# One core, a hybrid RWKV-7 / MLA / conv-Fourier / GQA network: where the scan's first inverse estimate is made, and where the norm work of the earlier pair stands

## The reference

```python
def step(S, inp):
    r_t, w_t, k_t, v_t, a_t, b_t = inp
    sa = jnp.einsum('bhij,bhj->bhi', S, a_t)
    S = S * w_t[:, :, None, :] + sa[..., None] * b_t[:, :, None, :] + v_t[..., None] * k_t[:, :, None, :]
    return S, jnp.einsum('bhij,bhj->bhi', S, r_t)
...
mean = jnp.mean(y, axis=-1, keepdims=True)
var = jnp.mean(jnp.square(y - mean), axis=-1, keepdims=True)
y = ((y - mean) * lax.rsqrt(var + GN_EPS)).reshape(B, L, D_INNER)
y = y * ln_w.astype(jnp.float32) + ln_b.astype(jnp.float32)
```

## Time and profile before

| | us |
|---|---|
| median of 3 runs | 2484.78 (2483.58 to 2485.72) |
| the profiled execution | 2485.72 |
| its span, first to last instruction | 2482.9 |
| PE busy in the span | 2190.2 (88%) |
| DVE, ACT, POOL busy | 1329.2, 838.6, 1201.1 |

### The profile page before, as it was taken

One profiled execution on the slowest core, in us unless ns is written; L12 is line 12 of the kernel. 1 busy time (PEld: TensorE's weight loads), 2 busy tenths in 40 slices (PEclk: granted clock), 3 DMA queues, 4 the chain that ended last, 5 costly groups with the idle time before them and its releaser, 6 DMA issues.

```text
span 2482.9 us, 57378 instructions
## 1 busy us (share of the span) xinstructions
PE 2190.2 (88%) x22614; PEld 1847.4 (74%) x22614; DVE 1329.2 (54%) x1932; ACT 838.6 (34%) x2187; POOL 1201.1 (48%) x708
## 2 busy tenths in 40 slices
PE   6799999989999999986948989999894999798876
PEld 4698999888888888876948947777693876565655
DVE  6766666664665566655264314454316082548645
ACT  1623323335566656553021223323202111212331
POOL 1266666552233223318847802231583897775234
PEclk8899999999999999996969999999896999899998
DMA  2233334355234323422201210100121221121001
GB/s 88 87 136 145 137 144 166 143 174 96 65 70 88 88 64 69 88 90 78 93 34 69 93 51 35 34 17 34 35 92 71 99 87 43 60 76 60 18 0 68
DMA packets 158909, 197.61 MB, mean 80 GB/s; under 512 B 120992, under 2 KB 123296, under 8 KB 156448
## 3 DMA queue, kind: packets, MB, share of 16 engines
q1 hardware_dynamic: 158752, 195.25, 25.2%
HBM read 156.24 MB, written 38.99 MB: 79 GB/s over the span
## 4 chain that ended last, share of the span: by engine, by line
PE 55%; DVE 8%; issue 7%; ACT 4%; POOL 3%; DVEq 0%; ACTq 0%; POOLq 0%
PE wide L803 8%; PE wide L1233 8%; PE wide L1234 8%; PE wide L1235 8%; PE wide L1710 5%; PE wide L1819 2%; PE wide L818 2%; PE wide L1595 1%; PE wide L1775 1%; PE wide L1803 1%; PE wide L826 1%; PE wide L820 1%; PE wide L2072 1%; POOL x_w L1092 1%; DVE normed L1371 1%
## 5 line engine op out<-in xcount | busy, mean ns | idle before, releaser
L1233 PE MATMUL wide<-mixed_high,w_high_rwkv_in 128*128 128x264 f32 x720 | 212.2, 295 | 29.0 <-ACT log_decay L435 20.1
L1092 POOL TENSOR_TENSOR x_w<-n,masks 128x192 f32<-128x192 f32 x48 | 28.7, 599 | 381.5 <-ACT n L969 381.5
L1235 PE MATMUL wide<-mixed_high,w_low_rwkv_in 128*128 128x264 f32 x720 | 206.6, 287 | 0.0
L1234 PE MATMUL wide<-u_low_second,w_high 128*128 128x512 f32 x464 | 185.5, 400 | 0.0
L1257 POOL TENSOR_TENSOR w_high<-weights,con 128x1024 fp32r<-128x1024 f32 x60 | 147.5, 2458 | 73.7 <-PE wide L1235 63.8
L1350 DVE TENSOR_TENSOR sq_sum<-sq_sum,squares 128x528 f32<-128x528 f32 (+1 forms) x54 | 87.3, 1617 | 178.3 <-ACT squares L1315 178.3
L355 PE MATMUL wide<-mixed_in,weights 128*128 128x264 f32 x672 | 159.1, 395 | 13.3 <-DVE mixed_in L325 12.3
L1233 PEld LDWEIGHTS wide<-mixed_high,w_high_rwkv_in 128*128 128x128 f32 x720 | 138.2, 192 | 37.1 <-ACT log_decay L435 26.3
L1260 POOL TENSOR_TENSOR w_low<-weights,w_high 128x1024 fp32r<-128x1024 f32 x60 | 157.6, 2627 | 4.7
L355 PEld LDWEIGHTS wide<-mixed_in,weights 128*128 128x128 f32 x672 | 129.1, 194 | 40.7 <-issue 9.5
L531 POOL TENSOR_TENSOR w_high_rwkv_in<-weights,con 128x1024 fp32r<-128x1024 f32 x45 | 108.3, 2406 | 71.7 <-PE wide L1235 71.0
(11 more groups left out here) (327 smaller groups left out, 6520.5 us busy)
## 6 DMA issues: line engine op xcount, KB each, us to landing
weights<-in_stream SPq DMA_DIRECT2D x200, 512.0 KB, 3.4
forms<-form SPq DMA_DIRECT2D x16, 2020.5 KB, 6.3
forms_in<-forms SPq DMA_DIRECT2D x96, 144.0 KB, 4.5
forms_in<-forms SPq DMA_DIRECT2D x32, 288.0 KB, 4.4
gate_bonus<-forms SPq DMA_DIRECT2D x16, 576.0 KB, 4.1
r_ahat_r<-forms SPq DMA_DIRECT2D x32, 144.0 KB, 3.5
mixed<-gate_bonus SPq DMA_DIRECT2D x14, 264.0 KB, 2.1
gated<-mixed SPq DMA_DIRECT2D x14, 264.0 KB, 5.0
```

The lines of the kernel that those rows point to most:

```text
L1233: pe.matmul(dst, w[0], x[0], start=start, stop=False)
L1234: pe.matmul(dst, w[0], x[1], start=False, stop=False)
L1235: return pe.matmul(dst, w[1], x[0], start=False, stop=stop)
```

## The change

The item W is gone. The first estimate of W is now made on DVE, in an item `start` for each group: the masked block 0 of `b_and_k` plus the unit matrix, one addition of 64 rows by 192 for each head. Its semaphore `w_start` so counts two for each group. The first XW now waits for X itself (`x_start`). In the list, centre stands ahead of the pass, square and norm behind the last `start` and ahead of the first E, and M and post are put one behind each E from level 0 on. POOL makes the small n_levels ahead of X.

```diff
         def schedule(inv, scan, post):
             rest, filler = [], []
+            if post:
+                rest += [("centre", 0, 0)]
             if inv:
-                rest += [("G", 0, 6), ("N", 0, 6), ("G", 1, 6), ("N", 1, 6), ("G", 2, 6), ("N", 2, 6), ("G", 3, 6), ("W", 0, 3), ("G", 4, 3), ("W", 1, 3)]
-                late = [("E", (0, 0), 3), ("W", 2, 3), ("E", (0, 1), 3), ("E", (0, 2), 3)]
+                rest += [("G", 0, 6), ("N", 0, 6), ("G", 1, 6), ("start", 0, 0), ("N", 1, 6), ("G", 2, 6), ("start", 1, 0), ("N", 2, 6),
+                         ("G", 3, 6), ("G", 4, 3), ("start", 2, 0)]
                 filler += [("M", g, 3) for g in range(GROUPS)]
             if post:
+                rest += [("square", 0, 0), ("norm", 0, 0)]
                 filler += [("post", n, 4) for n in range(2)]
             if inv:
                 for lv in range(LEVELS):
-                    rest += late if lv == 0 else []
                     for g in range(GROUPS):
-                        rest += [("E", (lv, g), 3)] if lv else []
-                        if (lv or g == GROUPS - 1) and filler and (filler[0][0] == "M" or lv > 2):
-                            rest += filler[:1]
-                            filler = filler[1:]
+                        rest += [("E", (lv, g), 3)] + filler[:1]
+                        filler = filler[1:]
                     rest += [("XW", (lv, g), 3 if lv == LEVELS - 1 else 6) for g in range(GROUPS)]
-                    if post:
-                        rest += {0: [("centre", 0, 0)], 1: [("square", 0, 0), ("norm", 0, 0)]}.get(lv, [])
...
-                elif item == "W":
-                    group(odd_bank[arg % 2], of(x), lambda c: eye[:], grp(arg), w_mm)
...
                 elif item == "E":
-                        pe.wait_ge(q["w_start"], GROUPS * i + g + 1)
+                        pe.wait_ge(q["w_start"], 2 * (GROUPS * i + g + 1))
...
                 elif item == "XW":
+                    if lv == 0:
+                        pe.wait_ge(q["x_start"], 6 * i + 2 * g + 2)
...
-                elif item == "W":
-                    wait_heads(act, w_mm, W_MADE + GROUPS * i + arg + 1)
-                    act.activation(xw[:, W_OF + par_, flat(arg)], odd_bank[arg % 2][:, 0:GC * C], ACT.Copy).then_inc(q["w_start"], 1)
...
+                elif item == "start":
+                    dve.wait_ge(q["b_k_made"], B_K * i + b_k_done(arg))
+                    for hd, rows in enumerate(HEAD_ROWS):
+                        dve.tensor_tensor(xw[rows, W_OF + par_, flat(arg)].rearrange("p (c n) -> p c n", c=GC), b_k[rows, par_, hd, grp(arg), 0, :],
+                                          eye[rows].unsqueeze(1).to_broadcast([C, GC, C]), ALU.add).then_inc(q["w_start"], 1)
...
+                levelled(g, 0, 1)
                 x = xw[:, X_OF + par_, flat(g)].rearrange("p (c n) -> p c n", c=GC)
...
-                levelled(g, 0, 1)
```

More of the change, by code:

```diff
@@ L625, in program @@
             "g_mm", "n_mm", "m_mm", "e_mm", "xw_mm", "a_mm", "u_mm", "s_mm", "y_mm", "y_turned"))
-        w_mm, W_MADE = (s["in_rounded"], s["in_rest"]), SPLIT * KD
         def wait_heads(eng, done, count):
@@ L765, in schedule @@
                 for lv in range(LEVELS):
-                    rest += late if lv == 0 else []
                     for g in range(GROUPS):
-                        rest += [("E", (lv, g), 3)] if lv else []
-                        if (lv or g == GROUPS - 1) and filler and (filler[0][0] == "M" or lv > 2):
-                            rest += filler[:1]
-                            filler = filler[1:]
+                        rest += [("E", (lv, g), 3)] + filler[:1]
+                        filler = filler[1:]
                     rest += [("XW", (lv, g), 3 if lv == LEVELS - 1 else 6) for g in range(GROUPS)]
-                    if post:
-                        rest += {0: [("centre", 0, 0)], 1: [("square", 0, 0), ("norm", 0, 0)]}.get(lv, [])
                 rest += [("A", g, 3) for g in range(GROUPS)]
-            elif post:
-                rest += [("centre", 0, 0), ("square", 0, 0), ("norm", 0, 0)]
             rest += filler
@@ L873, in pe_pass @@
                                 mm.then_inc(n_mm[hd], 1)
-                elif item == "W":
-                    pe.wait_ge(q["x_start"], 6 * i + 2 * arg + 2)
-                    if arg < 2:
+                elif item == "M":
+                    if arg == 0:
                         pe.wait_ge(q["v_rows"], 2 * GROUPS * (i + 1))
-                    else:
-                        pe.wait_ge(q["w_start"], GROUPS * i + 1)
-                    group(odd_bank[arg % 2], of(x), lambda c: eye[:], grp(arg), w_mm)
[L881 to L884, removed]
+                    if arg == 2:
                         pe.wait_ge(q["m_rows"], GROUPS * i + 1)
@@ L1039, in dve_pass @@
                             dve.wait_ge(q["x_start"], 6 * i + 2 * g + 2)
-                            dve.wait_ge(q["w_start"], GROUPS * i + g + 1)
+                            dve.wait_ge(q["w_start"], 2 * (GROUPS * i + g + 1))
                     chunks, m = live(g, lv), width_of(live(g, lv))
```

## The result

| | median us | runs |
|---|---|---|
| before | 2485.25 | 4 (2483.58 to 2487.49) |
| after | 2552.24 | 4 (2550.65 to 2557.18) |

The ratio is 1.0272, with a 95% interval of 1.0254 to 1.0290: 67 us slower. The forecast was 36 us slower, 2521, and its range ended at 2545. The sign was right, the size was not, and the time lies outside the range.

The account below looks back on a forecast made before the run. PE's row of matmuls was taken to bound each scan pass. A net 2.4 us for 14 passes (34 us) plus 2 us for passes 0 and 1 gave 36 us slower, 2521; range 2484 to 2545.

Parts of the forecast that it names:

- A granted clock under 1.00 in the stage would be a cost that I don't count.: In the wkv7 scan: a lower granted clock would cost extra; left out of the sum, no size given.
- two holes of 1.6 and 1.9 us, and one at the head: PE waits 1.6 us ahead of E(0,2), 1.9 ahead of walk part 1, and from 971.9 to 973.5 before E(0,0).
- PE's records fall by 576, its busy time with them: In the profile after: PE has 576 fewer records and less busy time, while the span grows.
- W gone, 1.6 us a pass.: In each scan pass: dropping W's transposes and copies saves 1.6 us counted alone, some 26 us in all.
- item 2: Head of the pass: E(0,0) waits for DVE's last masks until 973.5, giving back most of W's saving.
- Start blocked by POOL.: Level 0, group 2: both start halves wait behind POOL's large n_levels, so PE waits 1.6 us at E(0,2).
- The norm behind it.: Level 0: y_var waits behind start, ACT's u comes late, PE idles 1.9 us; lag at E(1,0) 2.7 us.
- Later.: Rest of the pass: level-2 stall gone, 0.5 us saved; posts in level 1 add 0.2; centre hidden.
- A: Group 2's first start half gets ahead of POOL's large instruction, the second waits; 2498 us, chance 0.20.
- B: Start additions slip between POOL's instructions and are not held up; 2476 us, faster, chance 0.15.
- C: Late y_rows, centre holding G masks and gates holding XW add 1.5 us a pass; 2542 us, chance 0.07.

Follow-up runs that it names:

- early_poolwait: The changed kernel, with POOL waiting for all six start additions of the pass before its three large n_levels; 2489.89 us, 1.0004 of before.
- late_poolwait_m: late_poolwait with M of groups 0 and 1 moved ahead of E(0,0); 2482.83 us, 0.9975 of before.
- late_poolwait: late_contended with POOL waiting for the start additions before its large n_levels; 2491.98 us, 1.0011 of before.
- after_fill: The changed kernel with 24 unread matmuls ahead of E(0,2) and 24 ahead of the walk part that waits for u; 2529.55 us, 1.0158 of before.
- late_fill: late_contended with 36 unread matmuls ahead of E(0,2); 2523.69 us, 1.0140 of before.
- late_contended: The changed kernel with centre, square, norm, M and post back at before's places; 2548.86 us, 1.0229 of before.

## Why the prediction was wrong

The mechanism was right and the step that failed is its last sentence: "A granted clock under 1.00 in the stage would be a cost that I don't count." It was counted at nothing, and it is 1.1 of the 2.7 points: 1.0272 falls to 1.0158 when the holes are filled, 28 us. With the clock held, what is left is 1.6% against the 1.45% (36 us) forecast. With the 28 us in it the forecast would have been 2549, for 2552 measured; part of that closeness is luck, since the terms below err both ways. The forecast put two holes of 1.6 and 1.9 us, and one at the head, into a row whose longest wait was 0.63 (ahead of the N item at 967.42; the prediction names only 0.39, 0.17 and 0.43), and gave no case to what the clock does about them:

```profile
967.42 0.94 PE L871 MATMUL wide<-forms_in 64*128 64x128 f32 x12 [0.63 <-ACT u_and_v L971]
```

The sign "PE's records fall by 576, its busy time with them" held for the records alone (22614 to 22038): over the whole run PE's busy time rose from 2190.2 to 2213.5 us.

By its steps:

1. *W gone, 1.6 us a pass.* True of the instructions (36 records less a pass), but counted alone, as the prediction says; item 2 took most of it back. Early_poolwait has neither W nor the block, and it gains nothing.
2. *The head.* E(0,0) 9.8 us into the pass: measured 9.79. The work of W was cover for DVE's masks. Late_poolwait_m bears that out: with two M in that place the hole and the falls behind it are gone, 1.0011 to 0.9975. The passes between have 1.19 in place of 0.88 ahead of E(0,0).
3. *Start blocked by POOL.* Foretold to the instruction: the pair of group 2 alone, 3.74 us for 3.7 foretold (973.4 to 977.1), E(0,2) 13.47 into the pass for 13.4. Too small were only the pairs of groups 0 and 1, 1.0 to 1.1 us for the 0.6 taken, since one half stands behind POOL's short instructions (0.64 to 0.75 for 0.34 us); nothing waits there.
4. *The norm behind it.* y_var at 13.45 into the pass, ACT idle 3.68 ahead of Sqrt, the walk part at 15.13 for 15.65, as ACT's Sqrt and copies ahead of it overlap: their starts are 0.2 us apart. The hole there is 0.75 and not 1.9: 0.5 of the difference is that earlier start, and PE, whose group for E(0,2) takes 0.91 us at 1.2 GHz where one takes 0.52 at 2.4, comes later to it. E(1,0) came at 20.3 for 19.5: the clock's first cost. But this step was given too much of the cause. With the norm late the ratio is still 1.0229, and the order without M between the E has its own larger hole of 2.13 in place of the two. What part of step 4 is the norm's alone these kernels don't separate.
5. *Later.* The level-2 stall is gone as foretold. The posts cost more than the 0.2 taken: DVE waits 2.10 for ACT's y_ln ahead of the gates, and PE 0.46 in turn for DVE's state:

```profile
1038.39 0.44 PE L812 MATMUL wide<-state,r_ahat_r 64*128 64x64 f32 x4 [0.46 <-DVE state L1002]
```

The rivals: A (DVE first, one half short) and B (not held up) both fail on the 3.74 us: both halves are long, 1.36 to 1.94 us, in each of the sixteen passes, though the margin was 0.16 us here. The Trainium skill, "SBUF — State Buffer", section "Who interferes with whom", has the later of the two fully blocked, and the trace agrees with that: DVE is the later, and the pair ends only when two POOL instructions have. C's mechanism, the lag feeding itself through y_rows, has at most a small part: E(0,0) comes at 9.79 into the pass, as foretold without it, and the wait that it named at the gates costs PE 0.46.

What stays open: how the clock's fall comes about. In the pass shown it begins at 1023.9, behind idle times of 0.64, 0.25, 0.35 and 0.88 us on PE and 0.7 us before the 1.50. So the long hole can't have begun it there; it can at most have kept it up. But the same head, without the long hole, brings a fall in two of 13 passes in early_poolwait and in six in late_poolwait, and with the long hole filled in three (after_fill) and one (late_fill). So neither the head nor the long hole explains the falls alone. What the runs do show is that a row of PE with these holes had falls, that filling some of the holes took most of them away, and what they cost.

## What to carry to other kernels

Before work is moved off a saturated TensorE, ask what that work was covering: here it hid DVE's last masks, and something that needs no new input must take its place. Keep a DVE instruction with two SBUF inputs, such as the start additions, clear of GpSimd's (POOL's) long ones by letting GpSimd wait: here that took back 2.7 points, and in the full passes of early_poolwait PE waited for none of GpSimd's later results (in late_poolwait_m for 0.2 us in some). And where a change opens holes of one or two microseconds in a row of matmuls whose longest was 0.63, give the granted clock a case and a price of its own.

## What the runs showed of the hardware

In this stage PE's row with holes at the head (0.25 to 1.2 us) and longer ones behind it had 1.2 GHz for 3.4 to 10.2 us in each of the passes 2 to 14 of after and late_contended, though PE was busy 88% of the time in after (457.55 of 519.60). With the holes at the head alone, 1.2 GHz came in two and in six of 13 passes (early_poolwait, late_poolwait), and with the last of those filled in none (late_poolwait_m). Twelve records cost 0.64 us at 1.2 GHz for 0.35 at 2.4. Matmuls whose result nothing reads, put into the long holes, gave back 1.1 and 0.9 points.

DVE's two halves of 64 rows, 340 ns each when alone, took up to 1936 ns beside back-to-back GpSimd instructions of 1.85 us (5.56 for three): the first half waited for the rest of the one that was running, the second for the whole of the next.
